# Two-layer diffusion backbone: the up projection of layer 2's first feed-forward block by Strassen's seven products

## What is computed

```python
D_MODEL = 1024; SEQ = 512; CTX_LEN = 256; DEPTH = 2; D_FF = 2816

def modulation(cond, w_mod, b_mod):
    m = jax.nn.silu(cond) @ w_mod + b_mod
    return jnp.split(m, N_MOD, axis=-1)

def swiglu(h, w_up, w_down):
    a, b = jnp.split(h @ w_up, 2, axis=-1)
    return (jax.nn.silu(a) * b) @ w_down

for l in range(DEPTH):
    x = x + 0.5 * g1 * swiglu(modulate(x, nw[0], sh1, sc1), ffn1_up[l], ffn1_down[l])
    ctx = ctx + 0.5 * cg1 * swiglu(modulate(ctx, nw[0], ch1, cs1), ffn1_up[l], ffn1_down[l])
    # token mixer: pooling branch and gated linear attention, one output projection
    ...
    x = x + 0.5 * g3 * swiglu(modulate(x, nw[2], sh3, sc3), ffn2_up[l], ffn2_down[l])
return rmsnorm(x, final_norm_w)
```

## Time and profile before

| what | value |
|---|---|
| runs | 2952.67 to 2953.66 us, median 2953.64 |
| profiled execution: span from first to last instruction | 2951.5 us, 1.2 to 2.2 us below the runs |
| mean granted clock of TensorE | 0.995 of full speed |
| busy PE, DVE, ACT, POOL | 98%, 53%, 28%, 8% |
| matmuls | 16288 |
| read from HBM | 270.95 MB, mean 93 GB/s |

### The profile page before, as it was taken

The page is one execution under the profiler, slowest core; times in us unless marked ns, Lnnn a source line. Parts: engine busy times, 40 slices in busy tenths (PEclk is TensorE's granted clock), DMA queues, the critical chain, the costliest instruction groups (busy, mean ns, idle before and its releaser), DMA issues.

```text
span 2951.5 us, 41576 instructions
## 1 busy us (share of the span) xinstructions
PE 2901.9 (98%) x16288; PEld 2480.3 (84%) x16288; DVE 1551.8 (53%) x2567; ACT 828.2 (28%) x1171; POOL 248.5 (8%) x256
## 2 busy tenths in 40 slices
PE   7999999999999999999999999999999999999998
PEld 6888888888888888888888888888888678888886
DVE  4677677566333357767765762222237644533334
ACT  4211211253332242112112421121235343432223
POOL 1000000113500030000000200000021500200000
PEclk9999999999999999999999999999999999999999
DMA  8343335221112224444342432222113123333332
GB/s 255 115 121 114 114 114 146 74 67 44 36 51 64 75 79 143 114 136 121 115 136 72 122 93 59 63 64 62 57 52 82 46 68 96 93 96 97 99 93 79
DMA packets 460241, 274.81 MB, mean 93 GB/s; under 512 B 14122, under 2 KB 458324, under 8 KB 460116
## 3 DMA queue, kind: packets, MB, share of 16 engines
q1 hardware_dynamic: 457908, 269.08, 32.0%
q10 hardware_dynamic: 2208, 4.00, 0.4%
HBM read 270.95 MB, written 2.10 MB: 93 GB/s over the span
## 4 chain that ended last, share of the span: by engine, by line
PE 92%; DVE 4%; ACT 3%; issue 1%; DMA 0%; SPq 0%; ACTq 0%; POOL 0%; DVEq 0%; POOLq 0%
PE ps L1330 55%; PE ps L1337 28%; PE ps L1543 2%; PE ps L1369 2%; PE ps L1548 1%; PE ps L741 1%; PE ps L721 1%; ACT hhi L1696 1%; DVE hlo L1932 1%; ACT whi L1631 1%; DVE wlo L1836 0%; PE ps L709 0%; DMA first_mod<-in_w_mod 0%; DVE macc L1850 0%; DVE htmp L1922 0%
## 5 line engine op out<-in xcount | busy, mean ns | idle before, releaser
L1330 PE MATMUL ps<-hhi,whi 128*128 128x512 f32 x3136 | 889.7, 351 | 1.2 <-ACT whi L1631 1.2
L1330 PE MATMUL ps<-hlo,whi 128*128 128x512 f32 x3136 | 880.8, 348 | 0.0
L1836 DVE TENSOR_TENSOR wlo<-wraw,whi 128x1024 fp32r<-128x1024 f32 x371 | 456.3, 1230 | 592.3 <-ACT whi L1631 589.4
L1631 ACT ACTIVATE whi<-wraw 128x1024 fp32r<-128x1024 f32 x371 | 391.2, 1055 | 925.1 <-PE ps L1337 897.6
L1337 PE MATMUL ps<-hhi,wlo 128*128 128x512 f32 x3136 | 627.2, 349 | 0.0
L1330 PEld LDWEIGHTS ps<-hhi,whi 128*128 128x128 f32 x3136 | 501.3, 188 | 83.9 <-issue 3.7
L1337 PEld LDWEIGHTS ps<-hhi,wlo 128*128 128x128 f32 x3136 | 499.6, 188 | 82.1 <-issue 3.2
L1330 PEld LDWEIGHTS ps<-hlo,whi 128*128 128x128 f32 x3136 | 501.3, 188 | 79.6 <-issue 0.5
L1850 DVE SCALAR_TENSOR_TENSOR macc<-modraw,cond,macc 128x256 f32<-128x256 f32 x896 | 366.5, 481 | 0.1
L1330 PE MATMUL ps<-mhi,whi 128*128 128x512 f32 (+1 forms) x1184 | 334.5, 349 | 4.2 <-DVE mlo L2111 2.9
L1330 PE MATMUL ps<-mlo,whi 128*128 128x512 f32 (+1 forms) x1184 | 332.7, 348 | 0.0
(11 more groups left out here) (206 smaller groups left out, 2204.8 us busy)
## 6 DMA issues: line engine op xcount, KB each, us to landing
wraw<-in_ffn_up SPq DMA_DIRECT2D x176, 512.0 KB, 3.8
modraw<-in_w_mod SPq DMA_DIRECT2D x64, 1024.0 KB, 5.2
wraw<-in_ffn_down SPq DMA_DIRECT2D x64, 512.0 KB, 4.1
wraw<-in_w_in SPq DMA_DIRECT2D x64, 512.0 KB, 4.0
wraw<-in_ffn_down SPq DMA_DIRECT2D x32, 384.0 KB, 3.4
first_mod<-in_w_mod SPq DMA_DIRECT2D x8, 1024.0 KB, 11.7
wraw<-in_w_out SPq DMA_DIRECT2D x16, 512.0 KB, 3.9
wraw<-in_w_br_pool SPq DMA_DIRECT2D x16, 256.0 KB, 2.8
```

What stands on the lines that cost most here:

```text
L1330: nc.tensor.matmul(o, whi[:, slot, k, :], a[:, k * NT + t0:k * NT + t0 + n], start=(k == 0 and a is hi), stop=False)
L1631: nc.scalar.activation(whi[:, slot2], wraw[:, slot4], ACT.Copy).then_inc(hi_split, 1)
L1836: nc.vector.tensor_tensor(wlo[:, slot2], wraw[:, slot4], whi[:, slot2].bitcast(F32), ALU.subtract).then_inc(lo_split, 1)
```

## The change

In 20 of the 22 up pairs of layer 2's first feed-forward block, a pair's product is written as a 2 x 2 by 2 x 2 product of blocks: the rows are the units of `a` and `b`, the inner blocks 4 chunks each (top and bottom), the columns two halves of 384 tokens. In place of the eight block products, seven are made (`fast_tensor`), each with 4 chunks x 3 matmuls of 128 x 384, 84 in a pair. The operands of four of them are sums of token blocks (`t_sums`, `t_his`, `t_los`; made once, in `hraw`, `thi_top`, `thi_bottom` and `tlo`) and sums of weight blocks (`fast_sums`; made for each pair, `ssum` and `wsum`). Each operand is split into high part and rest as before (`fast_hi`, `fast_lo_term`); the weights' rests are written into the raw buffer itself (`wrest`), `slo` and `wlo`. The seven products go through four PSUM banks, out of which DVE builds the four results in between (`fast_vector`), and ACT takes the silu of each half (`fast_scalar`). The first two pairs of the block stay plain.

The block is cut in quarters of 6, 4, 6 and 6 chunks. It takes no modulation jobs any more. The second feed-forward block of layer 1 is cut in fifths of 4, 4, 4, 4 and 6 chunks, which gives it nine phases with four jobs each: 36 jobs, the 30 it had and the 6 of layer 2. The splits of the down units of the changed block, and of one unit of the mixer, are shortened to what was loaded. The buffer `att` is cleared in both mixers.

```diff
+QUARTERS = ((0, 6), (6, 4), (10, 6), (16, 6))
+FIFTHS = ((0, 4), (4, 4), (8, 4), (12, 4), (16, 6))
+FAST = {(1, 0): 2}
+FAST_TERMS = 7
...
+def groups_of(layer, ffn):
+    return {(0, 1): FIFTHS, (1, 0): QUARTERS}.get((layer, ffn), THIRDS)
...
-                if s == len(slots) - 1:
+                if s == len(slots) - 1 or (layer, ffn) in FAST:
                     room = 0
...
+            def fast_tensor(ph):
+                unit_at_start = ph["unit"] + 2 * ph["plain"]
+                for j in fast_pairs(ph):
+                    q, unit, p = fast_at(ph, j)
+                    pe.wait_ge(pair_free, p - 1)
+                    for r, which in enumerate((0, 1, 2, 3, 2, 3, 0)):
+                        out = fast_bank(p, which)
...
+                        if q == 0 and r in (1, 2, 3, 5):
+                            pe.wait_ge(t_lo, (0, 1, 2, 3, 0, 4)[r])
+                        if r == 4:
+                            pe.wait_ge(fifth_read, q + 1)
+                        if r == 5:
+                            pe.wait_ge(seventh_read, q + 1)
+                        if r == 6:
+                            pe.wait_ge(first_kept, q + 1)
+                        for k in range(DC // 2):
+                            for n, h in enumerate(fast_moving(r, k)):
+                                nc.tensor.matmul(out, quarter(unit_at_start, r)[:, k, :], h,
+                                                 start=(r < 4 and k == n == 0), stop=False, skip_group_check=True)
...
+                        for k in range(DC // 2):
+                            mm = nc.tensor.matmul(out, fast_lo_at(unit_at_start, unit, r)[:, k, :], fast_moving(r, k)[0],
+                                                  start=False, stop=k == DC // 2 - 1, skip_group_check=True)
...
+                            if fast:
+                                if fast is ph:
+                                    t_his()
+                                for r in range(FAST_TERMS):
+                                    fast_hi(fast, fast["plain"], r)
                             if kind == "up":
                                 act.wait_ge(w_used, unit + 2)
...
+                            if fast:
+                                fast_sums(fast, fast["plain"], range(3))
+                                if fast is ph:
+                                    t_sums(3 * l + 2 * ph["ffn"])
+                                    t_los((2, 1))
+                                fast_lo_term(fast, fast["plain"], 0)
+                                fast_sums(fast, fast["plain"], (3,))
+                                fast_lo_term(fast, fast["plain"], 1)
```

More of the change, by code:

```diff
@@ L106, in add_ffn @@
         parts = LATENT if end else BOTH
-        for t, (_, n) in enumerate(THIRDS):
-            add("up", layer, n, ffn, t, jobs[2 * t], parts=parts)
+        groups = groups_of(layer, ffn)
+        plain = FAST.get((layer, ffn))
+        for t, (_, n) in enumerate(groups):
+            add("up", layer, n, ffn, t, jobs[2 * t], parts=parts,
+                plain=None if plain is None else plain if t == 0 else 0)
             add("down", layer, DC // 2, ffn, t, jobs[2 * t + 1], parts=parts,
-                ahead=BOTH if t == len(THIRDS) - 1 and not end else None)
+                ahead=BOTH if t == len(groups) - 1 and not end else None)
     left = DEPTH * MODJ - START_JOBS
-    slots = [n for _, k in THIRDS for n in (k, DC // 2)]
     for layer in range(DEPTH):
@@ L494, in last_norm_out @@
     def last_norm_out(ph):
-        return (ph["kind"] == "down" and ph["third"] == 2) or ph["kind"] == "out"
+        return (ph["kind"] == "down" and ph["third"] == len(groups_of(ph["layer"], ph["ffn"])) - 1) or ph["kind"] == "out"
     norm, sq_count, used_count, split = 1, 0, 0, 0
@@ L538, in m_base @@
     def m_base(l, ffn, third=0):
-        hidden = sum(n for _, n in THIRDS)
-        return hidden * (2 * l + ffn) + DC * (l + ffn) + sum(n for _, n in THIRDS[:third])
+        return HIDDEN * (2 * l + ffn) + DC * (l + ffn) + sum(n for _, n in groups_of(l, ffn)[:third])
     def m_base_merge(l):
@@ new lines, in stmp_of, with mtmp_of, fast_next @@
+    def stmp_of(ph, h):
+        return stmp_fast if is_fast(ph) else stmp[:, h]
+    def mtmp_of(ph, h):
+        return mtmp_fast[:, h] if is_fast(ph) else mtmp[:, h]
+    def fast_next(ph, i, h):
+        if not isinstance(i, int) or not is_fast(ph):
+            return None
+        n = 2 * i + h + 1
+        if ph["kind"] == "up":
+            return ph if n == ph["plain"] else None
+        nxt = plan[plan.index(ph) + 1] if n == ph["pairs"] else None
+        return nxt if nxt is not None and nxt["kind"] == "up" and nxt["plain"] == 0 else None
@@ new lines, in fast_pairs, with fast_at, fast_unit, loaded @@
+    def fast_pairs(ph):
+        return range(ph["plain"], ph["pairs"]) if ph["plain"] is not None else range(0)
+    def fast_at(ph, j):
+        return ph["fast"] + j - ph["plain"], ph["unit"] + 2 * j, ph["pair"] + j
+    def fast_unit(unit):
+        return any(ph["unit"] + 2 * ph["plain"] <= unit < ph["unit"] + ph["units"] for ph in plan if ph["plain"] is not None)
+    def loaded(unit):
+        if isinstance(unit, int):
+            for ph in plan:
+                if ph["kind"] == "down" and is_fast(ph) and ph["unit"] <= unit < ph["unit"] + ph["units"]:
+                    return slice(0, groups_of(ph["layer"], ph["ffn"])[ph["third"]][1]), slice(0, P)
+                if ph["kind"] == "proj" and unit == ph["unit"] + 2:
+                    return slice(0, DC), slice(0, 3 * LOW)
+        return slice(0, DC), slice(0, P)
```

342 lines of the change are left out of this document (306 added, 36 removed).

## The result

The changed kernel takes 2961.47 us (median of seven runs, 2956.54 to 2963.88); the kernel before, measured beside it on the same chip, takes 2952.99 us (2949.80 to 2954.39). The ratio is 1.0028 with an interval of 1.0017 to 1.0038. That is slower by 0.28%: within the range of the prediction (2942 to 2970), but 6 us above its number, and on the slower side of the 0.2% inside which its likeliest case lay. The profiled execution has a span of 2959.7 us, 8.2 more than before, at a mean granted clock of 0.991 in place of 0.995.

The account below looks back on a forecast made before the run. It took PE to bound the kernel, busy 98% of the span; -47.5 + 7.4 + 0.4 + 37.8 + 0.8 + 3.0 = +1.9 us on 2951.5 gave 2953.4, or 2955.5 us on the median's footing. Range: 2942 to 2970.

Parts of the forecast that it names:

- likeliest case: Whole kernel: 2955.5 us, no change that a measurement would tell, a gain and a loss of over 40 us each; chance 0.45.
- Term A: Layer 2's 20 fast up pairs: 84 matmuls of 384 take 14.57 us a pair in place of 16.95; -47.5 us.
- second rival: Fast pairs: DVE's late subtraction makes PE wait for the sixth product's bank, 0.7 us a pair; 2969.5 us, chance 0.17.
- Term B: Before layer 2's first fast pair: DVE's 14 us of token sums and rests stretch that pair to 22.0 us; +7.4 us.
- DVE gets there at -11.6: Start of the fast part: DVE begins three weight sums 11.6 us before PE ends the second plain pair.
- term E: Small things: four more batches of modulation sums on PE, +0.8 us; shortened splits, cleared attention buffer, smaller row buffer, 0.
- Term C: Phase borders of layer 2's changed block: 1.25 us lost once waiting for mlo in place of 0.86; +0.4 us.
- Term D: Layer 1's second feed-forward: DVE's 12.1 us bodies outlast PE's 8.5, four down phases of 43.4 us against 33.9; +37.8 us.
- first rival: Layer 1's small down phases: DVE's lateness does not reach PE, only the wait for mlo; 2926.5 us, chance 0.20.
- Term F: Clock: PE's idle gaps in the small down phases and first fast pair bring half-clock stretches; +3 us, between 0 and 14.
- more than six stretches, with up phases longer than 68 us behind them: Sign that the forecast is wrong through the clock: more than six half-clock stretches, up phases behind them over 68 us.
- third rival: Clock: every gap in the small down phases brings the lower level outside the slack, 13.6 us for 3; 2966, chance 0.10.

Follow-up runs that it names:

- bank freed late: Against the change: in every fast pair VectorE makes the next pair's first weight rest before the subtraction that frees the sixth product's bank; 2972.30 us.
- Fifths alone: Against the change: layer 1's second block in fifths with all 36 jobs, no seven products, layer 2 cut as before without jobs; 2992.11 us.
- short multiply-adds: Against the change: in layer 1's second block a job's multiply-adds cover 32 of 256 columns, same instructions and transfers issued; 2925.48 us, measured once.

## Why the prediction came out as it did

| term | forecast, us | measured, us |
|---|---|---|
| A, seven products | -47.5 | 20 x (16.95 - 14.68) = -45.4 |
| B, start of the fast part | +7.4 | -34.6 + 45.4 = +10.9 |
| C, borders of layer 2 | +0.4 | -2.0 (the down phases) |
| D, E and F, fifths, sums, clock | +41.6 | 40.7 + 3.0 - 0.3 = +43.3 |
| elsewhere | 0 | +1.4 |
| sum | +1.9 | +8.2 |

**Term A held in kind and missed by 2.1 us.** The 84 matmuls of 128x384 run every 0.173 to 0.174 us, as interpolated, and the old pair's 16.95 us is the one of the earlier trace rows. A fast pair takes 14.68 us in place of 14.57, of which 0.06 is the bank: with the third sum moved behind the subtraction it takes 14.62. The layout of DVE's order named the right place, and the run with the bank freed late shows that its 0.2 us of margin was in truth about none. The second rival stood that near. By its rule of N/2.4 + 2.5 ns for a warm matmul, which the page gives for an isolated one, the Trainium skill ("TensorE: Matmul & The Clock Gate", Back-to-back issue gap) has 162.5 ns for a matmul of 384 and 215.8 for one of 512; the trace shows 173 to 174, and 228 to 233, so here the measured neighbours were the better guide, for the saving above all.

**Term B is the step that failed: the mechanism was right, its size was not.** The failing sentence is "DVE gets there at -11.6": it starts its three weight sums at 1723.10, which is 7.6 us ahead of the second plain pair's end. The 4.0 us between are ACT's: the eight row shifts (4.14 us) that the change puts ahead of the first plain pair's silu. The layout did not have them, because it began with the second pair; they belong to the "smaller row buffer changes" that term E put at 0, as work beside PE's. From there on the token work is 4.0 us later, the token sums at +1.7 in place of -2.3, and the pair takes 25.6 in place of 22.0. The fifth and the sixth product start 18.1 and 21.4 us behind the plain pair's end, where the layout had 14.7 and 17.9. The three runs on the order show the cause: with the shifts out of DVE's way the phase is 3.3 us shorter; with them in front of the next split it is not.

**Term C has the wrong sign, and is 2.4 us off.** The down phases of the changed block take less than before, though their border costs are about as laid out (one wait of 1.0 us for `mlo_fast`, where before had one of 0.7 for `mlo`). In the two six-chunk phases with full work a matmul of 512 columns follows the last after 230 ns and one of 256 after 119, in the last down phase after 229 and 118; before, the same block had 233 to 234 and 119 to 120, and 231 and 119. That makes about 1.7 us (an estimate from these steps and 864 matmuls). Why is open. The shortened splits are a poor candidate: the 4-chunk phase, with the shortest of them, has 233 and 120, and the phase of the earlier trace rows at 1222.60, with full splits, has 230 and 119.

**Term D was right, by its own pieces.** For the phase at 1155.3 the prediction has 4.25 + 0.2 + 36.3 + 1.2 + 1.4 = 43.4 us, and the trace has 4.0 until the first body, 13.1 for the body with the wait for the slab (0.47) and two small operations that it did not count, 11.9 and 11.9 for the others, 1.3 for the split and the wait behind it, and 2.45 for the last rest products at half clock: 44.6. Only the last item is not DVE's, and its excess of 1.05 over the forecast belongs to the clock. PE's waits for `wlo` are 2.6 us in the mean and at most 3.3, not 3.6. (The upper bound is added up wrongly: 0.5 us more in each of three bodies of four phases gives 43.8, not 45.) Fifths alone (+41.7 us of span) and the short multiply-adds (a phase of 36.5 in place of 44.1) show it from both sides. The first rival, that DVE's lateness doesn't reach PE, is refuted by these two.

**Term F was too small in this profile, and differs between executions.** Forecast 3 us; in layer 1's second block it is about 5. The up phases have +3.0, of which 0.8 is term E, and the down phases 2.9 over term D. There are seven stretches of 3.4 us at the granted clock of 0.50, the 1.2 GHz level, in this block, and one of 6.8 us in the first fast pair, where 18 matmuls take 5.89 us of PE, 0.33 each, in place of 0.173. The slack of the bodies swallowed more than half of their cost. The sign "more than six stretches, with up phases longer than 68 us behind them" was met (68.0 to 69.1), but at a third of the price of 13.6 that the third rival put on it.

How many such stretches come is not fixed by the code. Five runs that change layer 2 alone have the same second block of layer 1 as after, with the same waits for `wlo` (19.1 us in eight in the run with the shifts behind the split):

| run | block, us | half-clock stretches |
|---|---|---|
| after | 607.7 | 7 |
| fifths alone | 607.4 | 7 |
| first high part earlier | 606.9 | 6 |
| shifts behind the first pair's silu | 605.5 | 6 |
| bank freed late | 605.4 | 6 |
| shifts behind the split | 600.9 | 4 |

So terms D to F together are 36.5 to 43.3 us over before's 564.3. The 1.7 by which the profile exceeds the forecast lies inside that spread, so one profile can't size term F by itself. The same goes for the 1.4 us elsewhere: the mixer of layer 1, up to its output projection, is alone +1.9 (412.2 against 410.3), and it takes 408.7 in the run with the shifts behind the split.

So no rival came true alone. The terms A, B and D to F together are 7.3 us dearer than forecast (2.1 + 3.5 + 1.7), C gives 2.4 back, and 1.4 lie elsewhere: 6.3 us, enough to pass the border of 0.2%. A's and B's parts come back in the run with short multiply-adds, whose code there is the same (88.1 us for six fast pairs, 106.1 for the first phase); those of D to F and elsewhere are within what the same code differs by. The prediction had priced places where an engine was just in time at nothing or near their lower bound (A at nothing for the bank, E at nothing for the row buffers, F at 3 of 0 to 14). Such errors don't cancel: an engine that is early gives nothing, one that is late costs.

## What to carry to other kernels

A transformation that saves matrix work needs room on the other engines, and the price stands where that room is taken: compare, per pair, PE's time after the cut with the other engine's fixed body (8.5 against 11.9 us here), and cut so that PE's part stays the longer (six chunks, 12.7 us). An engine with strict order that prepares a new stage is as late as the last thing it waits for in the stage before, so lay out both queues from one stage earlier than the new work begins. And when a wait goes, look at its next name before counting the gain: two of the three reorderings here moved a wait to another instruction and gave nothing.
